# One product set per batch for the sample scores of a two-layer decoder step, with pages loaded by eights into four slots

## What is computed

```python
def diff_attn_core(q, qpos, segs, lam):
    scale = DA_DK ** -0.5
    scores = []
    for k, v, kpos in segs:
        s = jnp.einsum('bqhcd,bkhcd->bhcqk', q, k).astype(jnp.float32) * scale
        scores.append(jnp.where(kpos[None, :] <= qpos[:, None], s, NEG))
    p = jax.nn.softmax(jnp.concatenate(scores, axis=-1), axis=-1)
    a = p[:, :, 0] - lam * p[:, :, 1]
    # o = sum over the segments of a @ v

k_past = cache_k[l][page_table]      # (8, 2048, 4, 2, 64) per layer
v_past = cache_v[l][page_table]      # (8, 2048, 4, 128) per layer
```

## Time and profile before

| | |
|---|---|
| median of three runs | 1801.79 us |
| the profiled execution | 1800.66 us |
| its span, first to last instruction | 1799.0 us |
| PE, matmuls | 1554.4 us busy (86%), 14606 matmul records |
| DVE | 645.2 us busy (36%) |
| ScalarE, GpSimd | 273.7 us, 158.2 us busy |
| mean granted TensorE clock | 0.932 of full speed |

### The profile page before, as it was taken

How to read it: one execution, slowest core, us unless ns; L and a number is a source line. 1 busy time by engine, 2 the same in 40 slices (tenths; PEclk the granted TensorE clock), 3 DMA queues, 4 the chain that set the end, 5 groups by cost and what they waited for, 6 DMA issues and landing times. The chain is left out here.

```text
span 1799.0 us, 35221 instructions
## 1 busy us (share of the span) xinstructions
PE 1554.4 (86%) x14606; PEld 855.3 (48%) x14606; DVE 645.2 (36%) x1500; ACT 273.7 (15%) x594; POOL 158.2 (9%) x218
## 2 busy tenths in 40 slices
PE   6999997677699999999599999966777989999990
PEld 3457775455345433333144677744554453333330
DVE  2223767665313400000232167576642152000004
ACT  2112331012001011110111133110110010110112
POOL 1000000220200000000200000012120000000002
PEclk9999998888798999999799999988888989999995
DMA  8431149887850699899651221689969029989974
GB/s 258 157 128 48 47 152 319 291 292 252 305 206 27 268 392 411 341 411 410 251 187 70 74 91 51 225 289 319 322 233 358 35 72 389 412 341 412 411 303 173
DMA packets 172372, 437.71 MB, mean 243 GB/s; under 512 B 23922, under 2 KB 23923, under 8 KB 172211
## 3 DMA queue, kind: packets, MB, share of 16 engines
q1 hardware_dynamic: 155650, 377.10, 56.8%
q0 software_dynamic: 16560, 58.34, 8.6%
HBM read 402.75 MB, written 32.64 MB: 242 GB/s over the span
## 5 line engine op out<-in xcount | busy, mean ns | idle before, releaser
L1048 PE MATMUL bank<-wslots,heads 128*32 128x512 f32 (+2 forms) x1088 | 266.2, 593 | 7.6 <-DVE heads L1837 3.8
L748 PE MATMUL bank<-xT,wslots 128*128 128x272 f32 x1024 | 243.5, 394 | 1.5 <-ACT heads L1321 0.8
L748 PEld LDWEIGHTS bank<-xT,wslots 128*128 128x128 f32 x1024 | 191.1, 190 | 42.7 <-issue 5.7
L1048 PE MATMUL bank<-hgrn,heads 128*32 128x512 f32 (+2 forms) x704 | 182.8, 593 | 0.0
L702 PE MATMUL bank<-wslots,xT 128*128 128x512 f32 x384 | 173.2, 605 | 5.3 <-DMA wslots<-in_w_in 3.6
L1963 DVE TENSOR_TENSOR temps<-temps,bank 128x512 f32<-128x512 f32 x24 | 16.5, 688 | 449.4 <-PE bank L1048 449.4
L1641 DVE STREAM_TRANSPOSE wslots<-wslots 128x1024 f32<-128x1024 f32 x128 | 153.4, 1226 | 4.5 <-DMA wslots<-in_cache_k 3.6
L1072 PE MATMUL bank<-wslots,temps 128*32 128x512 f32 (+2 forms) x544 | 141.3, 594 | 1.4 <-ACT temps L1404 1.4
L1048 PEld LDWEIGHTS bank<-wslots,heads 128*32 128x32 f32 (+2 forms) x1088 | 85.6, 127 | 117.0 <-issue 112.2
L806 PE MATMUL bank<-wslots,smalls 32*32 32x256 f32 x4096 | 108.4, 443 | 29.5 <-issue 15.4
L999 PE MATMUL bank<-wslots,xT 128*128 128x512 f32 x256 | 114.5, 608 | 3.8 <-DVE xT L1711 3.8
(11 more groups left out here) (319 smaller groups left out, 1727.8 us busy)
## 6 DMA issues: line engine op xcount, KB each, us to landing
wslots<-in_cache_k SPq DMA_DIRECT2D x256, 256.0 KB, 4.2
wslots<-in_cache_v SPq DMA_DIRECT2D x184, 256.0 KB, 4.5
wslots<-in_w_gate SPq DMA_DIRECT2D x20, 2048.0 KB, 13.6
wslots<-in_w_down SPq DMA_DIRECT2D x20, 2048.0 KB, 15.1
wslots<-in_w_up SPq DMA_DIRECT2D x18, 2048.0 KB, 15.9
wslots<-in_w_in SPq DMA_DIRECT2D x14, 2048.0 KB, 10.1
hgrn<-in_w_up SPq DMA_DIRECT2D x10, 2048.0 KB, 18.4
hgrn<-in_w_gate SPq DMA_DIRECT2D x10, 2048.0 KB, 16.3
```

What stands on the lines that cost most here:

```text
L748: x = mm(bank[6 + g % 2][:, 0:HALF], w[:, c, h * P:(h + 1) * P], xT[:, c, half * HALF:(half + 1) * HALF], start=(c == 0), stop=(c == DC - 1))
L1048: x = mm(bank[2 + k][a:z, :], xeT[T_ % 2][:, c, a:z], weights((what, l, e), DC)[:, c, :], start=(c == 0), stop=(c == DC - 1))
```

## The change

A batch is scored in one set of products. `batch_scores` takes the place of `unit_scores`: the same 64 products, each with 512 columns, which it reads from two ring places at once (`kring[r, u:z + 1:z - u, :, ...]`), so a layer has 8 sets in place of 16. The ring gets a fourth place, weight slot 0. Which place a unit goes to, and which batch has to be scored before it may be loaded there, stands in two tables, `UNIT_SLOT` and `UNIT_AFTER`. Place 0 takes unit 5 alone, after the last input projection; then it is the home of value quads, as before, which now wait for batch 2. The tables of slots (`SCORES`, `TURN_AT`, `VALUES`, `NEW_AT`) and the list of loads are written anew; the last batch stands at slot 98 (before, the last unit at 101), and the second half of the value quads begins at slot 107 (before 110). The last value quad's home is another one, so it waits for V28 (before, for V26).

```diff
-NU = 3
+UNIT_SLOT = (1, 2, 3, 1, 2, 0, 3, 1, 2, 3, 1, 2, 3, 1, 2, 3)
+UNIT_AFTER = (None, None, None, 0, 0, None, 1, 1, 2, 3, 3, 4, 4, 5, 5, 6)
...
-        kring = w_a[:, 4096:16384].rearrange("p (u g x) -> p u g x", u=NU, g=UNIT)
+        kring = w_a[:, :].rearrange("p (u g x) -> p u g x", u=4, g=UNIT)
...
-        SCORES = (0, 3, 6, 16, 21, 26, 31, 36, 39, 47, 55, 64, 74, 84, 93, 101)
...
+        SCORES = (0, 16, 24, 34, 45, 61, 79, 98)
...
+        VALUES = (45, 47, 49) + tuple(51 + 11 * k // 3 for k in range(13)) + tuple(107 + 2 * k for k in range(16))
...
+            order = [(0, q) for q in range(6)] + [(1, 0)] + [(0, q) for q in range(6, 12)]
+            late = [(SCORES[UNIT_AFTER[q // 2]] + (8 if q // 2 in (12, 14) else 0), 0, q) for q in range(12, NQ)]
+            late += [(SCORES[2], 1, v) for v in range(1, NV)] + [(VALUES[v - NV], 1, v) for v in range(NV, 19)]
+            late += [(VALUES[v - 7] if v >= 23 else VALUES[15], 1, v) for v in range(19, NQ)]
+            return order + [(kind, q) for _, kind, q in sorted(late)]
...
-                            if w < NU:
-                                sp.wait_ge(*last_use(("in", l, 3 + w)))
+                            if UNIT_AFTER[w] is None:
+                                sp.wait_ge(*last_use(("in", l, 6 if w == 5 else 3 + w)))
                             else:
-                                sp.wait_ge(sq_ps, UNITS * l + w - NU + 1)
+                                sp.wait_ge(sq_ps, DB * l + UNIT_AFTER[w] + 1)
...
-                pe.wait_ge(kt_ok, 4 * (UNITS * l + w) + 4)
+                pe.wait_ge(kt_ok, 8 * B + 8)
                 pe.wait_ge(qp_ok, B + 1)
...
+                u, z = sorted(UNIT_SLOT[2 * n:2 * n + 2])
...
-                            x = mm(bank[SCORE_BANKS[a]][32 * h:32 * h + 32, 256 * half:256 * half + 256], qp[r, q0:q0 + 32], kring[r, unit_of(w), :, c0:c0 + 32],
-                                   start=(i == 0 and half == 0 and d == 0), stop=(i == GB - 1 and half == 1 and d == 3))
+                            x = mm(bank[SCORE_BANKS[a]][32 * h:32 * h + 32, :], qp[r, q0:q0 + 32], kring[r, u:z + 1:z - u, :, c0:c0 + 32],
+                                   start=(i == 0 and d == 0), stop=(i == GB - 1 and d == 3))
```

More of the change, by code:

```diff
@@ L397, in build @@
         wl = [sem(f"w_loaded{i}") for i in range(7)]
-        kl = [sem(f"x_tile_then_k_quad_loaded{i}") for i in range(2 * NU)]
+        kl = [sem(f"x_tile_then_k_quad_loaded{i}") for i in range(6)]
         vl = [sem(f"v_quad_loaded{i}") for i in range(NV)]
@@ L441, in build @@
         FEAT_SLOTS = 15
[L442 to L447 removed]
+        SCORES = (0, 16, 24, 34, 45, 61, 79, 98)
+        TURN_AT = {t: 12 + x for x, t in enumerate((9, 10, 11, 12, 14, 15, 17, 18, 19, 20, 21, 22, 25, 26, 27, 28, 29, 30, 31, 32, 33, 34, 36, 37,
+                                                    39, 40, 41, 42, 46, 48, 50, 52, 55, 56, 57, 58, 62, 65, 67, 69, 73, 74, 75, 76,
+                                                    80, 83, 86, 88, 92, 93, 94, 95))}
+        SUM_UP = (SCORES[3] + 1, SCORES[7] + 1)
+        VALUES = (45, 47, 49) + tuple(51 + 11 * k // 3 for k in range(13)) + tuple(107 + 2 * k for k in range(16))
+        NEW_AT = (26, SCORES[7])
         ROWS_AT = (VALUES[15] + 1, VALUES[31] + 1)
[L449 removed]
+        V_HOME = tuple(v % 3 for v in range(16)) + (1, 2, 0, 3, 4, 5, 6, 1, 2, 0, 3, 4, 5, 6, 0, 5)
         NPAR = 13
@@ L460, in item, with unit_pages @@
             return ITEM_AT.get(s, (None, 0, 0))
-        def unit_of(w):
-            return w % NU
+        def unit_pages(w):
+            n = w // 2
+            in_order = UNIT_SLOT[2 * n] < UNIT_SLOT[2 * n + 1]
+            return n, 8 * (w % 2 if in_order else 1 - w % 2)
         loads = {}
@@ L476, in page_order, with quad_sem @@
         def page_order():
-            late = [(SCORES[q // 2 - NU], 0, q) for q in range(2 * NU, NQ)]
-            late += [(VALUES[v - NV], 1, v) for v in range(NV, 19)]
-            late += [(VALUES[v - 7] if v >= 23 else VALUES[15], 2, v) for v in range(19, NQ)]
-            early = [(0, q) for q in range(2 * NU)] + [(1, 0)] + [(0, q) for q in range(2 * NU, 4 * NU)] + [(1, v) for v in range(1, NV)]
-            return early + [(min(kind, 1), q) for _, kind, q in sorted(late) if (kind, q) not in early]
-        filled_to = [16 * int(c < NT) for c in range(2 * NU)] + [0] * NV
+            order = [(0, q) for q in range(6)] + [(1, 0)] + [(0, q) for q in range(6, 12)]
[3 more added lines that the diff above has]
+            return order + [(kind, q) for _, kind, q in sorted(late)]
+        def quad_sem(kind, q):
+            slot, half = (UNIT_SLOT[q // 2], q % 2) if kind == 0 else ((None, 0), (0, 0), (0, 1), (1, 0), (1, 1), (2, 0), (2, 1))[V_HOME[q]]
+            return 6 if slot is None else 7 + half if slot == 0 else 2 * (slot - 1) + half
+        filled_to = [16 * int(c < NT) for c in range(6)] + [0] * NV
         for l in range(L):
             for kind, q in page_order():
-                c = 2 * unit_of(q // 2) + q % 2 if kind == 0 else V_HOME[q] - 1 if V_HOME[q] >= NV else 2 * NU + V_HOME[q]
-                filled_to[c] += 64
-                loads[(l, kind, q)] = (c, filled_to[c])
+                filled_to[quad_sem(kind, q)] += 64
+                loads[(l, kind, q)] = (quad_sem(kind, q), filled_to[quad_sem(kind, q)])
         quad_loaded = kl + vl
@@ L637, in _ @@
                                 load_page(ids[j], vquad[V_HOME[q]][:, j].rearrange("p h n -> p (h n)"), t_in["cache_v"], quad_loaded[c])
-                    sp.wait_ge(sq_ps, UNITS * (l + 1))
+                    sp.wait_ge(sq_ps, DB * (l + 1))
+                    sp.wait_ge(pv_ps, vn(l, max(v for v in range(NQ) if V_HOME[v] in (3, 4))))
                     load_w(l * per + 7)
@@ L790, in od_turn, with batch_scores @@
                 x.then_inc(od_t, 1)
-            def unit_scores(l, w):
-                n, half = w // 2, w % 2
+            def batch_scores(l, n):
                 i, B = n % GB, l * DB + n
-                pe.wait_ge(kt_ok, 4 * (UNITS * l + w) + 4)
+                pe.wait_ge(kt_ok, 8 * B + 8)
                 pe.wait_ge(qp_ok, B + 1)
-                if i == 0 and half == 0:
+                if i == 0:
                     pe.wait_ge(sq_ok, 4 * (B // GB))
+                u, z = sorted(UNIT_SLOT[2 * n:2 * n + 2])
                 for d in range(4):
@@ L1639, in turn_pages @@
                 dve.wait_ge(quad_loaded[c], filled)
-                two = kring[:, unit_of(q // 2), 4 * (q % 2) + 2 * (x % 2):4 * (q % 2) + 2 * (x % 2) + 2, :].rearrange("p g n -> p (g n)")
+                two = kring[:, UNIT_SLOT[q // 2], 4 * (q % 2) + 2 * (x % 2):4 * (q % 2) + 2 * (x % 2) + 2, :].rearrange("p g n -> p (g n)")
                 tell(V.transpose(two, two), kt_ok)
@@ L1918, in _ @@
                         turn_pages(l, TURN_AT[s])
[L1919 to L1920 removed]
+                    if s - 4 in SCORES[:-1]:
+                        queries(l, SCORES.index(s - 4) + 1)
                     if FEAT_SLOTS + 2 <= s < FEAT_SLOTS + 2 + PT:
```

24 lines of the change are left out of this document (8 added, 16 removed).

## The result

The changed kernel takes 1787.88 us (median of four runs, 1783.47 to 1789.67) where the kernel before took 1801.57 beside it (1799.35 to 1802.73): a ratio of 0.9919, 95% interval 0.9902 to 0.9936, some 14 us less. The forecast was 1768.6, 33 us less: the sign was right and the size was not, by more than half. The profiled execution took 1789.67 us, its span is 1788.0.

What follows compares the result with a forecast made beforehand. The load list, its waits and PE's instruction packets were taken to bound the page stage nearly together; 15.7 us in layer 1 plus 17.5 in layer 0 gave 33.2 us less, 1768.6 us, range 1745 to 1797.

Steps and rivals of the forecast that it cites:

- The price of a set: Score products on PE: a merged set of 128 records takes about 3.7 us, with 5.5 us as the upper bound.
- The clock: Rival, chance 0.12: PE idles more between sets, and sets at the lower clock lose 3.3 us each; 1788 to 1801 us.
- DVE's turning ... hides behind the landing: Turning of key pages on DVE: the same 64 instructions, hidden behind the pages' landing, so nothing was added for it.
- The waits of the list: SP's list of loads: none of the old 21.6 us behind scores kept; new waits of 4.2 and 7 us added.
- unit 11: SP's list of loads: unit 11 must wait for batch 4, costing 7 us.
- The wait of unit 5: SP's list of loads: unit 5 must wait for the projection's end, costing 4.2 us.
- the waits behind value quads: SP's list of loads: 8 of the old 10.2 us behind value quads stay.
- The term of transfers: DMA loads from unit 3 to V15: 41 quads at the full rate of 2.73 us each, 111.9 us.
- The projection: Input projection at the stage's start: units 1 and 2 leave it, its one set grows; it ends 4.6 us earlier.
- Packets alone: Rival, chance 0.10: PE's instruction packets alone decide; six fewer, plus the projection, save 34 us a layer, 1734 us.
- the last rival: Rival, chance 0.10: loads released by whole batches leave SP's list dry; five stops total 44 us, 1836 us.
- Faster or not: Whole kernel: chance 0.84 of being faster by over 0.2%, 0.06 within that, 0.10 slower.

Runs made afterwards that it cites:

- the run with half the columns: Changed kernel with score products of the head dimension's second half cut to 64 of 512 columns: 1778.48 us, ratio 0.9849 of the kernel before.
- the runs with zeros: Changed kernel with four added products of zeros, 512 columns each, ahead of sets 2 and 3; that run alone: 1780.06 us, ratio 0.9862 of the kernel before.
- their control: Changed kernel with the same eight added products of zeros ahead of sets 2 and 3, but 32 columns wide: 1787.21 us, ratio 0.9915.
- the run with the last set first: Changed kernel with the last batch's set moved from slot 98 to 92, ahead of V14 and V15: 1786.39 us, ratio 0.9915.
- The run with two products: Changed kernel with every score product issued as two of 256 columns, one per ring place, all else kept: 1828.21 us, ratio 1.0145.
- zeros ahead of V3: Both edits (zeros; new tokens' scores at slot 22, batch 3's queries at 32) plus four zero products each ahead of V3 and V14: 1781.6 us, ratio 0.9894.
- the earlier new scores alone: Changed kernel with new tokens' scores at slot 22 (was 26) and batch 3's queries at slot 32 (was 28): 1779.16 us, ratio 0.9862.

## Why the prediction was wrong

**The price of a set was the first step that failed.** The prediction put a set at 3.7 us from eight rounds of 0.43 us, a row in which four products stand side by side. With sixteen a set takes 4.46 us at the upper clock, eight rounds of 0.56. Twice a unit's 5.5 us was the other bound; the truth lies in between. The prediction's own rows could have warned of the method: by the first round's 0.24 us eight rounds of a unit are 1.9 us, and the unit takes 2.76. The rule of the Trainium skill on packed tiles ("TensorE: Matmul & The Clock Gate", section "Measured speedup vs the span model") has them 10.6 times faster than one after the other. By the 0.43 us a record of the earlier trace rows the set here is 128 x 0.43 / 4.46 = 12.3 times faster, so the prediction's estimate from that rule, 5.2 us, was too high by about as much as its 3.7 was too low.

**The clock** was a rival with a chance of 0.12, and it is the largest part of this error: the eight sets cost 45.3 us where eight of 3.7 would be 29.6, a difference of 15.7 us. Of the 15.7, 6.1 is the price at the upper clock (8 x 0.76), 7.6 is what sets 2, 3, 4, 5 and 7 took beyond 4.46 at granted clocks of 0.62 to 0.81, and 2.0 is set 6, at a clock of 1.00 with its stop by "issue". The forecast had a last score 145.6 us after the first set, and it came at 160.8, 15.2 us later. That 15.7 and 15.2 agree is no proof, for not all sets lie on the chain: if the 60 to 75% of the run with half the columns holds here, an estimate, 9 to 12 us of the 15.2 go with the price of sets. By the runs with zeros and their control, the clock in sets 2 and 3 alone costs 7 to 10 us of the time; the two sets themselves got 4.0 us shorter in layer 1 and 2.5 in layer 0, so a part of it is noise or shows elsewhere. That this rival's 1788 us was met is luck: it had three sets lose 3.3 us each to the clock, and the most that one lost is 2.3.

**"DVE's turning ... hides behind the landing" was wrong.** That was the second failing step. The new tokens' scores now stood behind a set that waits, DVE's in-order list behind them, and the turning of half of unit 6 and all of unit 7 behind that: batch 3 ended 54.5 us after the first set in place of the forecast's 48. Moved out of the way, it ends at 48.0 and the time falls by some 10 us; 1.7 us of it, in layer 1, come from set 3's clock. That 48.0 is the forecast's number is chance, for set 2 still took 6.7 us there. The prediction did ask, for SP and PE, what queues behind a waiting instruction; it didn't ask it of DVE, whose order the change rewrites as well. The trace of before had such a wait to show, from 1136 to 1298 us:

```profile
DVE smalls L1623 <- PE bank L806: 23.7, 5, 7.5
```

**The waits of the list were the third.** The forecast kept none of the old 21.6 us behind scores, "since what is released comes in fours of quads". Up to the load of V15 the list waited 25.7 us behind scores: 10.7 for unit 11, forecast at 7, and 15.0 in five other waits, forecast at nothing. The wait of unit 5 was forecast at 4.2 and measured at 5.0, the waits behind value quads at 8 and measured at 1.8. V15's load was issued by 142.7 us after the first set, not 134.8. The term of transfers, 41 x 2.73 us, did not bind as the sum has it: with half of each page of values the stage lost only 3.6 to 5.9 us. From V15's load to the last score 18.1 us passed, not 10.8: V14 and V15 ran 1.9 us each at a granted clock of 0.50, 5.3 us of the recurrence and the first outputs' turning stand between V15 and the last set, and the set took 5.7. That those pieces stand there costs little by itself, as the run with the last set first shows.

**The projection** came nearly as worked out: 23.4 us from first set to its end before, 19.3 now, 4.1 less, forecast 4.6. The dearer set, 0.76 us over the 3.7, accounts for the difference.

**Packets alone, as a rival, missed, but packets matter.** The run with two products puts merging at some 40 us; in layer 1's stage it is 18.5. The sets are 20.0 us longer there, of which 11.0 are stops by "issue" inside them and the rest the sets' own length and clock. The Trainium skill's rule that fetching instructions is hidden ("Runtime: NRT & Kernel Launch", section "Instruction fetch mechanics") does not fit those stops, if they are the fetch; that they are is argued from their rhythm and from their return with the instructions, and no row ties a stop to a packet. The forecast credited packets with nothing. The new order and release eat most of this: with two products the list waits 46.0 us behind scores in layer 1, much as in the last rival, and the kernel is 26 us slower than before; the merged products turn the sign. So the change is a loss of 26 and a gain of about 40, and the forecast saw neither at its size.

**Faster or not** was answered rightly, with a chance of 0.84, and the time fell by 14 us, inside the range of 1745 to 1797. A good part of that is luck. The forecast had all of its 33.2 us between the first and the last score, where the profiled execution gained 4.3, and took what follows as 0, where it gained 6.1.

Open: how much the lower clock costs in sets 4 and 5, since zeros ahead of V3 gave nothing that can be told, what shortens the part behind the last score, and whether the two edits can add in an order not tried. Three sets that ran at the upper clock stopped for their instructions instead (set 6 here, set 3 of layer 0 with the scores earlier, set 5 with more zeros); that a faster PE meets these stops more often would explain it in part, and no run tests it. The single edits, zeros alone and the earlier new scores alone, stand at 0.9862 (0.9837 to 0.9886) and 0.9862 (0.9832 to 0.9891) of the kernel before, both under the changed kernel's 0.9919 (0.9902 to 0.9936). The second adds no work and is the version to keep.

## What to carry to other kernels

Merging small products pays where PE stops for its own instructions, but look at what the merged piece waits for: one wait for twice the data left PE idle for 4.94 and 6.33 us here, and the sets behind ran mostly at the lower clock. Price a merged piece at the clock of its place, not at the best row. And when a piece that waits is moved, follow the in-order list of every engine it feeds: here a line on DVE of 0.2 us held six turnings of pages for 4.85 us.

## What the runs showed of the hardware

A set of 128 records of 32 x 32 weights and 512 columns, eight rounds of sixteen, takes 4.46 us at the upper clock, 0.56 us a round; with the second half of the set cut to 64 columns the set still takes 3.0 us, more than half. Where PE was kept busy with products of zeros for 3.6 us of a wait, the next set of layer 1 ran at the upper clock (1.00) although 1.40 and 2.90 us of idle time still lay between; behind 4.94 us without work the first of these sets took 6.78 us (0.62). Products of 32 columns, 0.4 us in all, in the same place did not do it (0.65). It is not sure: in layer 0 set 3 took 6.1 us at 0.71 behind the same zeros and 2.67 us of idle time. The higher clock doesn't always shorten a set: PE stopped by "issue" inside three sets that ran at 1.00, for 0.62 to 2.07 us.
